# One decoder layer on one core: residual kept in token layout, scale columns first, pw2 tile by tile, five rows repeated over the partitions by GpSimd

## The reference, cut to what matters

```python
c_act = silu(c)
mod = c_act @ ada_w + ada_b                        # (1, 6144)
sh1, sc1, g1, sh2, sc2, g2 = split(mod, 6)
h = rmsnorm(x, mix_norm_g) * (1 + sc1) + sh1
u = h @ pw1_w + pw1_b                              # (256, 2048)
u = u[:, :1024] * sigmoid(u[:, 1024:])
u = causal_depthwise_conv(u, dw_w) + dw_b          # 31 taps
u = silu(layernorm(u, ln_g, ln_b))
y = u @ pw2_w + pw2_b
x = x + g1 * y
h = rmsnorm(x, ffn_norm_g) * (1 + sc2) + sh2
logits = h @ router_w + router_b                   # (256, 32); top 4, softmax over them
x = x + g2 * moe(h)                                # w1 (32, 1024, 2048), w2 (32, 1024, 1024), both float32
out = rmsnorm(x, final_norm_g)
```

## Time and profile before

| what | value |
|---|---|
| time, median of 3 (range) | 1175.99 us (1170.95 to 1177.86) |
| profiled execution, its own time | 1175.84 us |
| span of that execution | 1174.0 us |
| busy, share of the span | PE 85%, DVE 30%, ACT 14%, POOL 1% |
| HBM read, mean rate | 455.79 MB, 389 GB/s |
| chain that ended last, by engine | PE 52%, DMA 34%, SPq 5%, DVE 4% |

### The profile page before, as it was taken

The page is one execution under the profiler, slowest core; times in us unless marked ns, Lnnn a source line. Parts: engine busy times, 40 slices in busy tenths (PEclk is TensorE's granted clock), DMA queues, the critical chain, the costliest instruction groups (busy, mean ns, idle before and its releaser), DMA issues.

```text
span 1174.0 us, 21008 instructions
## 1 busy us (share of the span) xinstructions
PE 994.6 (85%) x7636; PEld 468.4 (40%) x7637; DVE 354.4 (30%) x952; ACT 163.5 (14%) x360; POOL 8.1 (1%) x21
## 2 busy tenths in 40 slices
PE   5999988898999787999887999887899887878755
PEld 3776663334443333444323344323444322332322
DVE  3788555221222222132222123212112322222222
ACT  2333252101001101011110011010111010101002
POOL 1000000000000000000000000000000000000000
PEclk9999997998989998989998989998989989898978
DMA  9985964999999999999999999999999999999995
GB/s 356 285 346 190 392 247 172 420 421 421 422 372 424 422 422 422 421 392 424 422 422 422 422 417 399 421 422 421 423 421 392 422 422 422 422 422 422 422 421 228
DMA packets 84441, 457.24 MB, mean 389 GB/s; under 512 B 9183, under 2 KB 29783, under 8 KB 30622
## 3 DMA queue, kind: packets, MB, share of 16 engines
q1 hardware_dynamic: 83088, 456.16, 95.6%
q10 hardware_dynamic: 1326, 0.71, 0.2%
HBM read 455.79 MB, written 1.05 MB: 389 GB/s over the span
## 4 chain that ended last, share of the span: by engine, by line
PE 52%; DMA 34%; SPq 5%; DVE 4%; issue 3%; ACT 1%; ACTq 1%; POOL 0%; DVEq 0%; POOLq 0%
DMA ring<-in_exp_w 34%; PE bank L1252 22%; PE bank L1275 11%; PE bank L1124 5%; SPq L298 5%; PE bank L1145 2%; PE bank L1231 2%; PE bank L1072 2%; PE bank L1108 1%; PE bank L1219 1%; PE bank L1229 1%; PE bank L1262 1%; PE bank L1243 1%; DVE scratch L904 1%; PE bank L1054 1%
## 5 line engine op out<-in xcount | busy, mean ns | idle before, releaser
L1252 PE MATMUL bank<-ring,xg 128*32 128x256 f32 (+2 forms) x3200 | 443.8, 481 | 58.9 <-DMA ring<-in_exp_w 58.4
L1252 PEld LDWEIGHTS bank<-ring,xg 128*32 128x32 f32 (+2 forms) x3200 | 168.0, 129 | 320.7 <-issue 175.6
L1275 PE MATMUL bank<-ring,actT 128*32 128x512 f32 (+2 forms) x1056 | 217.2, 615 | 22.7 <-DMA ring<-in_exp_w 14.6
L531 ACT ACTIVATE act<-scratch 128x128 f32<-128x128 f32 (+2 forms) x66 | 25.6, 388 | 766.3 <-DVE scratch L904 764.9
L1275 PEld LDWEIGHTS bank<-ring,actT 128*32 128x32 f32 (+2 forms) x1056 | 75.5, 133 | 140.4 <-issue 109.0
L904 DVE TENSOR_SCALAR scratch<-bank 128x128 f32<-128x128 f32 (+2 forms) x66 | 25.3, 384 | 312.6 <-PE bank L1252 312.6
L893 DVE SCALAR_TENSOR_TENSOR acc<-bank,gate,acc 128x512 f32<-128x512 f32 x136 | 93.0, 743 | 54.7 <-PE bank L1231 45.4
L923 DVE TENSOR_TENSOR ysb<-bank,g2half 128x512 f32<-128x512 f32 x29 | 20.1, 692 | 219.0 <-PE bank L1275 219.0
L1219 PEld LDWEIGHTS bank<-onehot_bf,arena 128*128 128x128 bf16 x1632 | 57.4, 102 | 23.0 <-issue 23.0
L1231 PE MATMUL bank<-ysb,onehotT 64*128 64x512 f32 x240 | 60.4, 615 | 2.9 <-DVE ysb L923 2.1
L1219 PE MATMUL bank<-onehot_bf,arena 128*128 128x32 bf16 (+2 forms) x1632 | 61.0, 195 | 1.0 <-DVE arena L833 1.0
(11 more groups left out here) (222 smaller groups left out, 515.2 us busy)
## 6 DMA issues: line engine op xcount, KB each, us to landing
ring<-in_exp_w SPq DMA_DIRECT2D x396, 1024.0 KB, 24.1
ring<-in_ada_w SPq DMA_DIRECT2D x24, 1024.0 KB, 10.2
ring<-in_conf_pw_w SPq DMA_DIRECT2D x12, 1024.0 KB, 11.9
acc<-in_x SPq DMA_DIRECT2D x1, 1024.0 KB, 4.9
out<-acc SPq DMA_DIRECT2D x2, 512.0 KB, 3.1
g2full<-in_ada_b SPq DMA_DIRECT2D x1, 512.0 KB, 4.3
xT<-in_final_norm_g ACTq DMA_DIRECT2D x1, 512.0 KB, 3.7
b1f<-in_exp_b SPq DMA_DIRECT2D x1, 256.0 KB, 3.7
```

The lines of the kernel that those rows point to most:

```text
L531: a.activation(act[:, h * c:(h + 1) * c], g_lim[h][:, 0:c], ACT.Sigmoid, scale=ALPHA).then_inc(sig_ready, 1)
L1252: ins = mm(up_to(m, n, r), xg[:, b, k, 0:m], wk[:, at:at + span(m)], start=False, stop=(k == KT - 1))
L1275: ins = mm(dst, actT[:, f % (2 * q), at:at + m], wk[:, f % 2 * D + r * H:f % 2 * D + (r + 1) * H], start=(f < sides), stop=(f >= KT - sides))
```

## The change

The residual x stays with tokens on partitions from beginning to end.

- *Start.* ACT sums the squares of x row by row, DVE puts 1/rms on the diagonal of `diag`, and the product of x with `diag` turns and normalises in one step (it stays in PSUM banks 3 to 6). c has a semaphore of its own and is turned first. The ada columns of sh1 and sc1 come in two halves: four chunks with the scale, then pw1 chunk 0, then four with the shift. Tile 0 of pw1 is made from x scaled but not shifted; the missing part, shift times pw1, is a product of its own (`sh1wide`), added to pw1's bias. From tile 1 on `hT` holds scaled and shifted x. The transfers of the depthwise weights are issued by ACT behind the copy of the scale row.
- *pw2.* The chunks hold 256 rows of `pw2_w` and all 1024 columns. The product has `conv` as weights and 512 columns moving: tile 0 of the tokens with both halves, then tile 1's first half, then its second.
- *Rows.* g1, the product of g1 and pw2's bias, sh2, a2 (scale of the second norm) and g2 are made as rows, and GpSimd repeats each over 128 partitions, in ten `partition_broadcast` of 512 columns. `pick` and its two products go.
- *Routing.* The logits come from x (turned by TensorE) times a router matrix scaled with a2 (`arw`), then times 1/rms and plus a row; each tile of 128 tokens is routed by itself, tile 0 between the halves of pw2's tile 1. h is made straight in token layout. Most of b1's split goes to ACT, the low parts all to DVE.

The diff, cut to its core:

```diff
-    stream = [("ada", k) for k in range(KT)]
-    for t in range(KT):
+    stream = [("scale", q) for q in range(4)] + [("pw1", 0)] + [("shift", q) for q in range(4)]
+    for t in range(1, KT):
         stream += [("pw1", t)]
...
             # sync: after chunk 11
-                    sp.dma_start(g2full[:, :], ada_b[0, 5 * D:6 * D].partition_broadcast(P)).then_inc(s_g2b, 16)
+                    for g in range(2):
+                        for j in range(4):
+                            at = (g + 1) * 2 * D + j * H
+                            sp.dma_start(ada_rows[g][32 * j:32 * j + 32, :],
+                                         ada_b[0, at:at + H].partition_broadcast(32)).then_inc(s_ab, 16)
...
             # gpsimd
+            def spread(to, row, landing):
+                for j in range(2):
+                    pool.partition_broadcast(to[:, j * H:(j + 1) * H], row[32 * j:32 * j + 1, :]).then_inc(landing, 1)
+            pool.wait_ge(s_row, 3)
+            spread(g1_row, modrow[0][0:64, :], s_rows1)
+            pool.wait_ge(s_gbias, 1)
+            spread(xb_row, gbias_row, s_rows1)
+            spread(sh2_row, modrow[0][64:128, :], s_rows1)
+            pool.wait_ge(s_row, 4)
+            spread(a2_row, modrow[1][0:64, :], s_rows2)
+            spread(g2full[:, :], modrow[1][64:128, :], s_rows2)
...
             # vector: from the first norm to the first taps
+            for t in range(TT):
+                v.tensor_scalar(diag[:, t, :], ident[:, :], frstd[:, t:t + 1], None, ALU.mult).then_inc(s_diag, 1)
+            v.wait_ge(p_row, 1)
+            column(sc1, P, AB + KT)
+            v.wait_ge(p_x, 1)
             for k in range(KT):
-                v.tensor_scalar(hT[:, k, :], hT[:, k, :], a1[:, k:k + 1], modcol[:, 0, k:k + 1],
+                v.tensor_scalar(hT[:, k, :], normed(k), a1[:, k:k + 1], None, ALU.mult).then_inc(s_h, 1)
+            v.wait_ge(p_row, 2)
+            column(sh1, P + KT, AB)
+            v.tensor_copy(sh1wide, sh1[:, :].unsqueeze(2).to_broadcast([P, KT, 32])).then_inc(s_sw, 1)
+            v.wait_ge(p_t0, 1)
+            for k in range(KT):
+                v.tensor_scalar(hT[:, k, :], normed(k), a1[:, k:k + 1], sh1[:, k:k + 1],
                                 ALU.mult, ALU.add).then_inc(s_h, 1)
...
+            v.wait_ge(p_corr, 1)
+            v.tensor_tensor(vcol[:, bass.ds(PB1, 2, 8)], bank[0][:, P + 16:P + 18], vcol[:, bass.ds(PB1, 2, 8)],
+                            ALU.add).then_inc(s_fix, 1)
...
             # vector: after the layer norm
+            v.wait_ge(s_rows1, 6)
+            for t in range(TT):
+                step(v.tensor_tensor(acc[:, t, :], acc[:, t, :], xb_row, ALU.add))
...
+            v.wait_ge(p_lrow, 1)
+            link(v.tensor_tensor(log_row[:, :], bank[0][:, 3 * P:3 * P + E], rb_row[:, :], ALU.add))
+            v.wait_ge(p_y, 1)
+            done = [gated_y(0, r) for r in range(2)]
             for r in range(2):
+                residual(0, r, done[r])
+            v.wait_ge(s_rows2, 4)
+            for r in range(2):
+                scaled(0, r)
+            base(0)
+            normed2(0)
+            for r in range(2):
+                modulated(0, r)
+            for r in range(2):
+                rest_of(0, r)
+            v.wait_ge(p_y, 2)
+            residual(1, 0, gated_y(1, 0))
+            scaled(1, 0)
+            logits(0)
+            choose(0)
+            for r in range(2):
+                low(0, r)
+            for r in range(2):
                 step(v.tensor_copy(g2half[64 * r:64 * r + 64, :], g2full[64 * r:64 * r + 64, r * H:(r + 1) * H]))
+            base(1)
+            v.wait_ge(used, CH_EXP)
+            residual(1, 1, gated_y(1, 1))
+            scaled(1, 1)
+            normed2(1)
+            modulated(1, 0)
+            modulated(1, 1)
+            logits(1)
+            choose(1)
+            rest_of(1, 0)
...
             # tensor: the first norm and the ada columns
+            half_row("scale", 0).then_inc(used, 1)
+            pe.wait_ge(s_diag, TT)
             for k in range(KT):
                 for t in range(TT):
-                    ins = tr(bank[2 + k // 2][:, (k % 2) * T + t * P:(k % 2) * T + (t + 1) * P],
-                             acc[:, t, k * P:(k + 1) * P], ident[:, :])
+                    ins = mm(bank[3 + k // 2][:, (k % 2) * T + t * P:(k % 2) * T + (t + 1) * P],
+                             acc[:, t, k * P:(k + 1) * P], diag[:, t, :], start=True, stop=True)
...
+            pw1_half(0, 0)
+            pw1_half(0, 1).then_inc(p_t0, 1)
+            for q in range(4):
+                ins = half_row("shift", q)
+            ins.then_inc(p_sh, 1)
             pe.wait_ge(s_dw, 16 * (2 * PE_STEPS + 1))
...
+            half_column(1, P + KT)
+            pe.wait_ge(s_sw, 1)
+            for k in range(KT):
+                j = k % 4
+                ins = mm(bank[0][32 * j:32 * j + 32, T:2 * T].rearrange("p (h n) -> p h n", h=2), sh1wide[:, k, :],
+                         w[:, :, k, :], start=(k < 4), stop=(k >= 4))
+            ins.then_inc(used, 5)
...
             # tensor: pw2 and the routing
+            def pw2(t, r, k):
+                w = w_slot(number["pw2", k // 2]).rearrange("p (a n) -> p a n", a=2)
+                return mm(bank[1 + 2 * t + r][:, :], conv[:, k, t * P:(t + 1) * P], w[:, k % 2, r * H:(r + 1) * H],
+                          start=(k == 0), stop=(k == KT - 1))
...
+                for r in range(2):
+                    ins = pw2(0, r, k)
+            ins.then_inc(p_y, 1)
+            for k in range(KT):
+                ins = pw2(1, 0, k)
+            ins.then_inc(p_y, 1)
+            pe.wait_ge(s_sh2w, 1)
+            for k in range(KT):
+                ins = mm(bank[0][:, 3 * P:3 * P + E], sh2wide[:, k, :], rw[:, k, :], start=(k == 0), stop=(k == KT - 1))
+            ins.then_inc(p_lrow, 1)
+            turn_x2(0, 0, 5)
+            turn_x2(0, 1, 6)
+            for k in range(4):
+                ins = pw2(1, 1, k)
...
+            route(0)
+            turn_x2(1, 0, 1)
+            for k in range(4, KT):
+                ins = pw2(1, 1, k)
...
+            turn_x2(1, 1, 2)
+            pe.wait_ge(s_logit, 1)
+            route(1)
```

More of the change, by code:

```diff
@@ L748, in _ @@
             centre(1)
-            rstd_out(2)
+            rstd_out(1)
             centre(2)
             centre(3)
+            v.wait_ge(s_ab, 16 * 12)
+            v.wait_ge(used, number["ada", 2 * KT - 1] + 1)
+            v.tensor_tensor(modrow[0], bank[6][:, :], ada_rows[0], ALU.add).then_inc(s_row, 1)
             v.wait_ge(s_cent, 4)
@@ L868, in _ @@
             either(v, w0, SIZES[0], lambda m: select(1, 0, m))
-            low(1)
-            low(3)
+            low(1, 0)
+            low(1, 1)
+            step(v.scalar_tensor_tensor(out=key[:, :], in0=counts, scalar=float(E), in1=tie[:, :],
+                                        op0=ALU.mult, op1=ALU.add))
+            step(v.tensor_scalar(over[:, :], counts, float(WIDE), None, ALU.is_gt))
+            step(v.tensor_scalar(over2[:, :], counts, float(WIDE + SMALL), None, ALU.is_gt))
+            v.wait_ge(s_b2, 32)
+            v.tensor_tensor(ysb[:, 0, :], b2f[:, :], g2half[:, :], ALU.mult).then_inc(y_ready, 1)
+            step(v.memset(gate4, 0.0))
             v.wait_ge(s_prob, TT)
```

618 lines of the change are left out of this document (306 added, 312 removed).

## The result

The changed kernel takes 1181.34 us, median of 8 runs (1177.69 to 1186.0), against 1176.35 for the kernel before in the same session (8 runs, 1170.95 to 1178.36): a ratio of 1.0050, 95% interval 1.0027 to 1.0072. It is 5.0 us slower where 4.8 us less was predicted, and lies above the predicted range (1165 to 1179). The profiled execution took 1180.65, its span is 1178.9.

A forecast was written before the change was run, and what follows sets the result against it. The end was taken to hang on the expert stream's start, set by the front's chain to `eidx`. Parts 0, -0.6 and -4.2 sum to -4.8 us, from 1175.84 to 1171.0; range 1165 to 1179.

The forecast's parts named there:

- What bounds the kernel: Expert stream: the end comes a fixed time after its start, which waits on the front's chain to the `eidx` write.
- Part one: Start to first taps, scale columns first: taps at 46.2 us as now, taken as 0; lower end -3.7.
- the diagonals at 10.6: Start of the front: x there at 5.8, then squares, table load, root and short DVE steps give diagonals at 10.6 us.
- the landing of the shift chunks: Front, first 10.4 MB of transfers: scale landed at about 15 us and shift at about 29.
- Part two: First taps to the start of pw2: ada chunks run without the turn of one row, -0.6 us.
- Part three: Start of pw2 to first expert transfer behind the wait: 60.4 us against 64.6 now, -4.2.
- The broadcasts: GpSimd's ten row broadcasts ahead of and beside pw2: 1.15 us each, hidden up to 3.2 each, so no cost.
- Rival (d): Broadcasts take over 3.2 us each; at 5 us each +13, 1189 us; chance 0.10, slower.
- Rival (c): Front: dw rows or shift chain come late by 4 to 8 us, 1175 to 1179; chance 0.15.
- Rival (e): Some twenty engine handovers counted as free cost 0.2 to 0.4 each: +4 to +8 us, 1175 to 1179; chance 0.07.

The follow-up runs named there:

- the last pair: Changed kernel, modulation in eight whole chunks again, TensorE waits filled in front and part three: with a final GpSimd iota 1172.78 us, without it 1181.38.
- the lone broadcast: Kernel before plus one unused partition_broadcast as GpSimd's last work: 1179.79 us (1.0034); with an iota behind it: 1174.76 (0.9992).
- the reordered, filled kernel: Changed kernel plus final GpSimd iota, diagonals and scale rows moved earlier, identity products filling TensorE's front waits: 1173.95 us (0.9989).
- the kernel with rows by DMA: Changed kernel with the ten broadcasts replaced by GpSimd transfers of the rows to DRAM and back: 1181.08 us (1.0052).
- the one-pass front: Changed kernel plus final iota, scale-columns-first undone (eight whole chunks, tile 0 made once): 1173.51 us (0.9982); front waits filled: 1173.65 (0.9980).
- The plain iota-last kernel: Changed kernel plus one unused GpSimd iota of 128x32 behind the ten broadcasts: 1174.72 us (0.9992).
- The two other kernels with the old part three: Kernel before plus one unused broadcast as GpSimd's last work, 1179.79 us (1.0034), and the same with an iota behind it, 1174.76 (0.9992).
- reordered, iota last: Changed kernel plus final GpSimd iota, with squares, root, diagonals and scale rows moved earlier in the front, no fillers: 1174.18 us (0.9992).

## Why the prediction was wrong

**What bounds the kernel** was read rightly. The end follows the first transfer behind the wait on `eidx`, within the scatter named above: +4.2 there, +4.9 in the span, and +8.7 there with +8.6 in the median for the last pair.

**Part one** is the step that failed: "I take 0 for this part", measured +8.51. Its sum began with "x is there at 5.8" and "the diagonals at 10.6", which need an identity before that (2.63 in the kernel before); it came at 12.94. The diagonals ended at 18.91 in the changed kernel and at 10.75 in the one that differs from it by the iota alone. The load is what the sum lacked, and the only place where I weighed it was in the middle of the kernel, ahead of the first broadcast. There it is indeed hidden: the first broadcast begins 0.15 us after its row is ready (129.86 + 0.68 to 130.69), and the MODIFY_POOL_CONFIG for it stands at 16.6, so the load had over 100 us of idle GpSimd. What costs is the way back, which the *next* execution pays, in front of the first instruction of the old library, where everything waits. The Trainium skill, GPSIMD Engine Reference, section 2.1 Instruction dispatch, gives about 6 us for the first call of freshly loaded code, without a visible instruction. The gaps ahead of the lone broadcast agree with it, 6.01 and 6.02 in the two kernels that have one. The way back to `iota` and `affine_select` took longer, 7.10 to 12.05, and there the measurement decides.

With the load gone the rest of part one came close at full clock: in the reordered, filled kernel scale rows end at 19.8 (19.2 predicted), tile 0 starts at 22.7 (22), the shift rows end at 33.85 (32.6), the taps start at 47.15 (46.2). What was mis-sized there is the landing of the shift chunks: "at about 29"; the last one was waited for until 32.56 in the kernel with rows by DMA, whose tile 0 had ended at 28.9, and until 32.79 here. (The sum also has a slip: 32.6 with 0.7, 1.0 and 0.9 is 35.2 and not 34.9; the column products end at 35.79 here.) Why they land later than 10.4 MB of traffic would give is open. So the order is worth +1.0 and not 0 at the taps, against the one-pass front's +0.15 with its waits filled too: scale columns first gains nothing there, and the medians (1173.95 and 1173.65) don't tell the two apart. The plain iota-last kernel shows +4.5 at its taps. Of the 3.6 that it is behind the filled, reordered one, 1.9 are there when the shift rows end (tile 0 took 10.10 instead of 7.14) and the rest comes from 38 to 45, at clock 0.83 and 0.82; the prediction's sum has no term for a lower clock. Of the 8.5, then, I estimate the load at about 7.5 (54.70 less 47.15) and the order at 1.0. These two kernels also differ in their fillers and in the order ahead of the diagonals. Where the iota alone differs, the load's price at the taps was 3.99 in the changed kernel, whose twin with the iota ran at the lower clock for a while, and 8.69 in the last pair.

**Part two**: -0.6 predicted, -0.73 measured. Right.

**Part three**: -4.2 predicted, -3.55 measured. With P0 for the start of pw2 as in the prediction, L930, the step that was L845, at P0+45.95 (45.9), L1037 at P0+53.6 (53.4), the end of L1062 at P0+59.4 (59.2), SP 1.66 behind it instead of 1.25. The steps were right; the profile that they were set against was a slow one of its kind. The two other kernels with the old part three show it in 62.86 and 62.87 where the kernel before shows 64.57, with the clock at 1.00 from 165 to 175, where before it had 0.66 up to 170. The new part three takes 60.0 to 62.7 in its ten profiles, 61.3 in the mean. So what it gains is 3.3 against the profile that it was set against and 1.6 against the other two, and 4.2 was too much by a reading from one execution.

**The broadcasts**: 1.15 taken, 1.05 measured in the mean; hidden with seventeen microseconds to spare. DVE's four multiplications (L803) beside them took 3.42 instead of 2.50, under cover. Rival (d), that they are long, is out. Rival (c), the dw rows late, is out: their turns start at 41.34, as the shift rows end, and so they do in the kernels without the gap (33.78 in the filled, reordered one); of its shift chain late by 4 to 8 there is the 1.0 above. Rival (e), the handovers, would have ended at 1179 and has neither the size nor the cause. No rival said that a cost of the broadcasts could stand at the other end of the kernel; that a new kind of instruction is not only its own duration was the hole in the list.

**What stays open**: when the clock falls is not shown. Waits of 0.8 to 1.7 us come before the falls of the front, and none of the four kernels with those waits filled fell there; yet three of the five with the unfilled waits of 0.81 and 1.14 kept 1.00 as well, and a filled one fell in 35 to 40. The profiles show one execution each, so that the fillers kept the clock up in the front is likely and no more. Nor is it shown why some medians gain less than their first transfers do (reordered, iota last: -3.3 there, -1.4 in the median); the profiled span has 983.9 behind that transfer, against 982.0 before, which is within the scatter.

## What to carry to other kernels

Ask of each new instruction on GpSimd whether the kernel's first ones still start at once: if GpSimd stands at the start of an execution with "issue" as the releaser, look for a MODIFY_POOL_CONFIG ahead of the gap and at what its program ends with, and end it with an instruction of the kind that it begins with, where the engine is idle anyway. One `iota` of 0.16 us turned 0.5% slower into no slower. And weight columns split in two halves that must both be in before the chain goes on didn't shorten the chain here; the half that came first gave TensorE early work with waits in it.

## What the runs showed of the hardware

- An execution starts with the GpSimd code that the last one ended with. MODIFY_POOL_CONFIG stands ahead of the first `affine_select` in all fourteen kernels, and also ahead of the broadcasts and of the `iota` behind them. Ahead of the selection it costs next to nothing where GpSimd's last work was an `iota`, a subtraction or transfers (selection at 2.09 to 2.57), and 10.83 to 12.05 us of idle time with "issue" behind it in the four kernels that end with a broadcast. A load in the middle of the kernel took 6.01 and 6.02 ahead of a lone broadcast, 7.10 ahead of the `iota` behind it, and 8.36 to 10.53 ahead of the `iota` behind ten broadcasts (seven kernels).
- A `partition_broadcast` of one row of 512 float32 to 128 partitions takes 0.73 us each in a row of them, 1.10 to 1.35 in the groups beside DVE's work.
- DVE is slower beside GpSimd's memset of 128x2304 and the constants ahead of it. Three casts of 32x32 take 2.74 or 2.75 us in the eleven kernels where they stand beside it (L643, 14.06 to 16.81, where the memset ends at 16.36) and 0.58 or 0.59 in the three reordered ones where they come after it; two diagonals take 3.45 beside it and 0.48 after it:

```profile
11.54 0.58 DVE L655 CAST bsel<-ident 32x32 bf16<-32x32 f32 x3
```

- The granted clock in the views doesn't show the slow start of TensorE: it reads 1.00 from the beginning in the changed kernel, yet the first eight products of L1139 took 1.94 us there and the 24 of the next group 2.78, so 0.93 for eight.
- GpSimd waited 15.8 us for its own small transfers to land, while SP's queue was moving 1 MB chunks.
